# Expert output of a PEER layer: each token's v sum on four strips of 256 columns in place of two of 512

## The reference, cut to what matters

```
u = jnp.take(u_tab, ib, axis=0)                                   # 128 rows of 1024 per token
coef = gb * jax.nn.gelu(jnp.einsum('cd,ced->ce', xb, u), approximate=False)
return jnp.einsum('ce,ced->cd', coef, jnp.take(v_tab, ib, axis=0)) # the v sum of each token
```

## Time and profile before

| | |
|---|---|
| runs (us) | 3550.49, 3573.14, 3546.98 |
| profiled execution | 3567.71 us, span 3566.0, mean granted PE clock 0.855 |
| PE busy | 2750.9 us, 77% |
| DVE busy | 2363.7 us, 66% |
| POOL busy | 1964.6 us, 55% |
| ACT busy | 531.5 us, 15% |
| DMA | 1246.47 MB, mean 350 GB/s; the gathers are 1073.87 MB of it |
| line 1325 on `e_v` alone | 2844 records, 817.3 us busy |
| chain of waits that ended last | PE 36%, DVE 17%, DMA 13%, unknown queue 13%, issue 11%, POOL 7% |

### The profile page before, as it was taken

One profiled execution on the slowest core, in us unless ns is written; L12 is line 12 of the kernel. 1 busy time (PEld: TensorE's weight loads), 2 busy tenths in 40 slices (PEclk: granted clock), 3 DMA queues, 4 the chain that ended last, 5 costly groups with the idle time before them and its releaser, 6 DMA issues.

```text
span 3566.0 us, 42043 instructions
## 1 busy us (share of the span) xinstructions
PE 2750.9 (77%) x15556; PEld 1288.3 (36%) x15556; DVE 2363.7 (66%) x6100; ACT 531.5 (15%) x1162; POOL 1964.6 (55%) x2093
## 2 busy tenths in 40 slices
PE   9899886888888889986756676667656777677787
PEld 7777762333323333333323332233223332222111
DVE  5678889676676657766787767867686756665200
ACT  3211311110111102111011101010111101111101
POOL 0013345555655566556665666666665666666663
PEclk9999997999999899998867786678767787798999
DMA  6559998999999999989999999999999999999996
GB/s 218 209 179 306 352 344 305 329 359 377 382 357 322 366 375 377 369 317 403 393 373 335 369 406 368 353 338 407 379 363 332 394 395 403 386 378 396 375 361 234
DMA packets 385293, 1246.47 MB, mean 350 GB/s; under 512 B 40512, under 2 KB 75072, under 8 KB 384320
## 3 DMA queue, kind: packets, MB, share of 16 engines
q0 software_dynamic: 294912, 1073.87, 79.8%
q1 hardware_dynamic: 90176, 169.91, 13.5%
HBM read 1216.75 MB, written 26.87 MB: 349 GB/s over the span
## 4 chain that ended last, share of the span: by engine, by line
PE 36%; DVE 17%; another core or an unknown queue 13%; DMA 13%; issue 11%; POOL 7%; ACT 2%; SPq 0%; POOLq 0%; DVEq 0%; ACTq 0%
PE e_acc L1325 9%; DVE e_u L2248 5%; PE e_pl L1413 5%; DMA e_v<-in_v_tab,e_idxT 4%; DMA e_u<-in_u_tab,e_idx 3%; PE e_pd L1201 3%; PE e_pd L1021 3%; PE e_pd L1227 3%; PE e_acc L1370 3%; POOL e_v L994 3%; PE e_acc L1395 3%; DVE e_late L2248 2%; POOL e_u L986 2%; DMA e_late<-in_v_tab,e_idxT 2%
## 5 line engine op out<-in xcount | busy, mean ns | idle before, releaser
L2248 DVE CUSTOM_DVE_ANT_0 e_u<-e_u,e_c 128x1024 f32<-128x1024 f32 x776 | 942.4, 1215 | 315.8 <-DMA e_u<-in_u_tab,e_idx 240.4
L986 POOL DMA_INDIRECT e_u<-in_u_tab,e_idx x776 | 745.7, 961 | 693.3 <-DVE e_dots L2248 274.6
L994 POOL DMA_INDIRECT e_v<-in_v_tab,e_idxT x711 | 675.6, 950 | 517.4 <-PE e_acc L1325 203.3
L1325 PE MATMUL e_acc<-e_v,e_wd 128*32 128x512 f32 x2844 | 817.3, 699 | 171.6 <-DMA e_v<-in_v_tab,e_idxT 115.0
L1413 PE MATMUL e_pl<-e_late,e_v 128*128 128x512 f32 x608 | 340.8, 658 | 46.5 <-DVE e_side L2058 17.2
L2248 DVE CUSTOM_DVE_ANT_0 e_late<-e_late,e_c 128x1024 f32<-128x1024 f32 x248 | 300.8, 1214 | 102.4 <-DMA e_late<-in_u_tab,e_idx 74.3
L1325 PE MATMUL e_acc<-e_late,e_wd 128*32 128x512 f32 x832 | 271.9, 731 | 73.5 <-DMA e_late<-in_v_tab,e_idxT 47.2
L986 POOL DMA_INDIRECT e_late<-in_u_tab,e_idx x248 | 237.1, 956 | 163.8 <-DVE e_dots L2248 106.2
L1325 PEld LDWEIGHTS e_acc<-e_v,e_wd 128*32 128x32 f32 x2844 | 113.6, 116 | 533.0 <-issue 266.9
L1968 DVE SCALAR_TENSOR_TENSOR e_gbc<-e_hc,e_cw,e_gbc 128x128 f32<-128x128 f32 x960 | 303.6, 344 | 1.5 <-issue 1.0
L994 POOL DMA_INDIRECT e_late<-in_v_tab,e_idxT x208 | 197.3, 948 | 133.2 <-issue 52.8
(11 more groups left out here) (299 smaller groups left out, 3249.4 us busy)
## 6 DMA issues: line engine op xcount, KB each, us to landing
e_u<-in_w_in SPq DMA_DIRECT2D x38, 512.0 KB, 3.9
e_v<-in_w_in SPq DMA_DIRECT2D x38, 512.0 KB
e_v<-in_w_in SPq DMA_DIRECT2D x76, 256.0 KB
e_u<-in_u_tab,e_idx POOLq DMA_INDIRECT x776
e_zb<-in_w_c SPq DMA_DIRECT2D x48, 256.0 KB
e_v<-in_v_tab,e_idxT POOLq DMA_INDIRECT x711
e_arena<-in_w_r SPq DMA_DIRECT2D x32, 256.0 KB
e_zb<-in_w_r SPq DMA_DIRECT2D x32, 256.0 KB
```

The lines of the kernel that those rows point to most:

```text
L986: pool.indirect_dma_start(out=rows_in[i], out_offset=None, in_=io["u_tab"], in_offset=bass.IndirectOffsetOnAxis(ap=idx[n % 2][:, j:j + 1], ...
L994: pool.indirect_dma_start(out=rows_in[i], out_offset=None, in_=io["v_tab"], in_offset=bass.IndirectOffsetOnAxis(ap=idxT[n % (LAG + 1)][:, ...
L1325: last = pe.matmul(acc[rows, cols], w[:, at_:at_ + 32], rows_in[row][:, cols], start=(step == 0), stop=True, skip_group_check=True)
L2248: dve.tensor_tensor_reduce(rows_in[i], rows_in[i], c[:, :], 1.0, 0.0, ALU.mult, ALU.add, dots[n % 2][:, j:j + 1]).then_inc(s_dot, 1)
```

## The change

Each token's sum is cut into four parts of 256 columns, and part h goes to strip `lane ^ h`. So a token uses all four strips, with four products and eight records in place of two and four. Parts 0 and 1 share the first bank, parts 2 and 3 the second; `begins` lets only the first product of a tile in each strip and bank start afresh. The number of wait instructions per token stays, except for a tile's first token, which has four in place of two. The strip sums become 11 instructions: one of 128x256, four of 32x256, two of 64x256, four of 32x256. `HALF_SUMMED` is 5 of them, `SUMMED` all 11; who waited for the first of three now waits for five, who waited for three waits for eleven.

```diff
--- before.py
+++ after.py
@@ -158,8 +158,14 @@
 LAG, V_LAG = 1, NSEL + V_HEAD
 CHUNKS = 2
 LOW, HIGH = slice(0, P // 2), slice(P // 2, P)
-SUM_ROWS = [((slice(0, P), slice(0, P)),), ((LOW, HIGH), (HIGH, LOW))]
-SUMS = [sum(len(r) for r in SUM_ROWS[:h]) for h in range(NH + 1)]
+STRIP = P // LANES
+PARTS = LANES
+PART_W = D // PARTS
+STRIPS = [slice(STRIP * i, STRIP * (i + 1)) for i in range(LANES)]
+SUM_ROWS = [((slice(0, P), slice(0, P)),), tuple((STRIPS[i], STRIPS[i ^ 1]) for i in range(LANES)),
+            ((LOW, HIGH), (HIGH, LOW)), tuple((STRIPS[i], STRIPS[i ^ 3]) for i in range(LANES))]
+SUMS = [sum(len(r) for r in SUM_ROWS[:h]) for h in range(PARTS + 1)]
+SUMMED, HALF_SUMMED = SUMS[PARTS], SUMS[PARTS // 2]
 TAIL_AT, TAIL_SPAN, EARLY_TAILS = 4, 20, NT - 1 - LAG
 IN_PLACE = EARLY_TAILS - 1
 
@@ -169,9 +175,9 @@
     return (P // LANES) * (k % LANES) + k // LANES
 
 
-def strip_of(lane, h):
-
-    return lane ^ (2 * h)
+def strip_of(lane, part):
+
+    return lane ^ part
 
 
 ROWS = UW + VW + LW + 2
@@ -712,7 +718,7 @@
                 sp.dma_start(xin, dram["h"][n]).then_inc(s_hhin, 16)
 
             def sum_store(n):
-                sp.wait_ge(s_hh, SUMS[NH] * (n + 1))
+                sp.wait_ge(s_hh, SUMMED * (n + 1))
                 sp.dma_start(dram["h2"][n], xin).then_inc(s_h2, 16)
 
             def tail_loads(m):
@@ -1265,7 +1271,7 @@
                 if m < IN_PLACE:
                     pe.wait_ge(s_tin, 16 * (m + 1))
                 else:
-                    pe.wait_ge(s_hh, SUMS[NH] * m + (SUMS[1] if m == NT - 1 else SUMS[NH]))
+                    pe.wait_ge(s_hh, SUMMED * m + (HALF_SUMMED if m == NT - 1 else SUMMED))
                 if m:
                     pe.wait_ge(s_gp, m)
                 else:
@@ -1273,7 +1279,7 @@
                     pe.wait_ge(s_w_tail, 16 * 3)
                 if m == NT - 1:
                     turned(tail_h(m), s_ttr, range(KT // 2))
-                    pe.wait_ge(s_hh, SUMS[NH] * NT)
+                    pe.wait_ge(s_hh, SUMMED * NT)
                     turned(tail_h(m), s_ttr, range(KT // 2, KT))
                 else:
                     turned(tail_h(m), s_ttr)
@@ -1301,6 +1307,13 @@
                 product(pt, w_proj, PLE // P, 0, out)
                 product(pt, w_proj, PLE // P, 1, out).then_inc(s_pps, 1)
 
+            begun = set()
+
+            def begins(n, strip, bank):
+                first = (n, strip, bank) not in begun
+                begun.add((n, strip, bank))
+                return first
+
             def add_tokens(n, j, together):
                 if j == 0:
                     if n == 0:
@@ -1310,21 +1323,22 @@
                     pe.wait_ge(s_wd, n * (NSEL // (QUARTER * LANES)) + j // (QUARTER * LANES) + 1)
                 step = j // LANES
                 w = wd[step // QUARTER % 2]
-                for h in range(D // HALF):
+                for h in range(PARTS):
                     if j == 0 and n:
-                        pe.wait_ge(s_hh, SUMS[NH] * (n - 1) + SUMS[h + 1])
-                    cols = slice(h * HALF, (h + 1) * HALF)
+                        pe.wait_ge(s_hh, SUMMED * (n - 1) + (HALF_SUMMED, SUMMED)[h * PART_W // HALF])
+                    cols = slice(h * PART_W, (h + 1) * PART_W)
                     for i in range(together):
                         m, lane = n * NSEL + j + i, (j + i) % LANES
                         row, turn, _ = V_ROWS[m]
                         if h == 0:
                             pe.wait_ge(s_row[row], 16 * turn)
                         strip = strip_of(lane, h)
-                        rows = slice(32 * strip, 32 * strip + 32)
+                        rows = STRIPS[strip]
                         at_ = (step % QUARTER) * P + 32 * lane
-                        last = pe.matmul(acc[rows, cols], w[:, at_:at_ + 32], rows_in[row][:, cols], start=(step == 0), stop=True,
+                        last = pe.matmul(acc[rows, cols], w[:, at_:at_ + 32], rows_in[row][:, cols],
+                                         start=begins(n, strip, h * PART_W // HALF), stop=True,
                                          skip_group_check=True)
-                        if h == D // HALF - 1:
+                        if h == PARTS - 1:
                             last.then_inc(s_vmm, 1)
 
             def front(n, s):
@@ -1766,7 +1780,7 @@
                     if m < IN_PLACE:
                         act.wait_ge(s_tin, 16 * (m + 1))
                     else:
-                        act.wait_ge(s_hh, SUMS[NH] * (m + 1))
+                        act.wait_ge(s_hh, SUMMED * (m + 1))
                     if m:
                         act.wait_ge(s_outd, 16 * m)
                     else:
```

## The result

The changed kernel takes 3591.36 us (median of 8 runs, 3579.12 to 3599.93); the kernel before, beside it, 3558.03 us (8 runs, 3546.98 to 3573.14). The ratio is 1.008, interval 1.0059 to 1.0101: a little slower, within the 1% that I had called no change, and 85 us above the forecast. The profiled execution took 3579.12 us, span 3577.2, against 3567.71 and 3566.0.

A forecast was written before the change was run, and what follows sets the result against it. PE's v-sum products were taken to pace first halves, DMA transfers second halves. Terms -59 - 10 + 20 + 5 = -44 us, from 3550.5 to 3506 us; range 3440 to 3590, the forecast's own 3470 to 3530.

The forecast's parts named there:

- What bounds the kernel: In first halves of a tile's v sum PE sets the pace (tiles 0 to 2); in second halves, full DMA engines.
- The token: A token alone on PE in the v sum occupies it for 0.54 us in place of 0.98, saving 45%.
- the forecast of a third or more: Busy time of the v sum's product line on PE falls by a third or more.
- "-59" for the first halves: First halves of the v sum: 45% of the 131 us that PE's product line has in the chain is saved.
- I let the two cancel: First halves: other engines close behind PE are offset by sums hidden in the chain's 19 to 32% without named releaser.
- I take no cost for either: PE's products: doubled weight loads (0.28 us per token) and handing out eight pairs (at most 0.35 us) are hidden.
- Second halves, -10: Second halves and after 3002 us: transfers set the pace, so 10 us saved in all, ends 0 and 70.
- The strip sums, +20: Tile ends on DVE: eleven sums in place of three cost 2.5 us more, 8 times, together 20 us.
- The clock, +5: First halves of tiles 0 to 2: PE's clock share falls by 0.02, costing 5 us in the chain.
- the second rival: First halves: DVE and the recurrence's hand-overs hold the pace anyway, sums worth 0 to 15 us, about 3560 us; chance 0.22.
- the fourth rival: Strip sums decide: 0.71 us each whatever the size, 45 us on the path, 3586 to 3596 us; chance 0.13.
- the third: First halves of tiles 0 to 2: clock falls from 0.92 to 0.72, about 3558, up to 3600 us; chance 0.10.

The follow-up runs named there:

- e7: The kernel before, unchanged, traced on a faster chip: 3353.92 us.
- e8: The changed kernel with each quarter cut into two products of 128 columns, sixteen records per token, on the slower chip: 3667.55 us, ratio 1.0294 to the kernel before.
- e3: Kernel before with quarters and eleven sums in tiles 0 to 2 only, halves and three sums from tile 3, on a faster chip: 3353.34 against 3353.11 us.
- e6: The changed kernel itself, traced on a faster chip: 3355.92 us, ratio 1.0006 to the kernel before.
- e4: Kernel before with two tokens taken together in every second slot, products and sums as before, on a faster chip: 3341.48 against 3353.11 us, ratio 0.9964.
- e5: Kernel before with two tokens taken together in the odd slot instead of the even one, on a faster chip: 3362.2 against 3354.57 us, ratio 1.0026.
- e1: Kernel before with only the strip sums cut into eleven instructions, products unchanged, on a faster chip: 3364.33 against 3353.11 us, ratio 1.0035.
- e12: Repeat of the kernel before with only the strip sums cut into eleven, on a faster chip again: 3363.39 against 3353.55 us, ratio 1.0032.
- e10: Kernel before with twice the records per token, still two strips and three sums, on the slower chip: 3583.9 us, ratio 1.0061.
- e2: Kernel before with twice the records per token, still two strips and three sums, on a faster chip: 3356.74 against 3353.11 us, ratio 1.0009.
- e11: Kernel before with two tokens taken together in every second slot, on the slower chip: 3597.21 us, ratio 1.0101.

## Why the prediction was wrong

1. **What bounds the kernel: wrong in the first halves, right in the second.** I read 341 to 358 GB/s beside a PE at 85% as PE's pace. e7 has the same PE work in the same stretch and 395 GB/s, so PE was no bound at that length. What holds down on chips B stays open. The earlier trace rows could not tell: their two largest entries, "another core or an unknown queue" and "issue", are together 27 to 61% of the first halves' chain, and in a trace that lacks over a quarter of the semaphore updates they mark in large part where the chain was lost. The prediction counted the unknown queue alone (19 to 32%), and took it for a place where more of PE's work was hidden. The trace doesn't exclude that, but the time shows no saving from it.
2. **The token: right.** 0.57 us from start to start for a forecast 0.54, 8192 records, PE's busy time on `e_v` down by 23% (the forecast of a third or more was for tokens alone, and these means hold the trickling ones). The price of a record in a burst was right as well: 0.0375 us in e8, under the 0.043 of the earlier trace rows. The Trainium skill, "TensorE: Matmul & The Clock Gate", section "Wait — 56ns, not 53.3ns?", has about 62 ns per matmul with hardware decode off. The prediction held against that, but 16 records don't test it: over 100 records e8's trace has 57 ns each, the time of wide products included, and no 256 in a row are faster than 59.8 ns each. The traces neither show nor exclude such a price in a long stream, and whether hardware decode was on no run shows.
3. **In the sum, "-59" for the first halves: the step that failed.** The six first halves gave -16 us in the first trace (-5, -1, -2, -5, -4, +1), and e3 gave 0.0 on chips A, the sums of three tiles included. "I let the two cancel" was the choice: what was unnamed was not a hidden store of PE's work. On chips A the transfers take the saving, shown by e6 against e7; on chips B the saved work is idle time of PE, 166 us of it, and what PE then waits for is known in part only. What a spared PE is worth by itself no run isolates: e4 gains 12 us on chips A, and e5, with as little PE work, loses 8.
4. **"I take no cost for either", of loads and of handing out records: the second step that failed, on chips B.** On chips A twice the records are +3.6 us, within their interval of nothing; on chips B 0.61%, 22 us. The earlier trace rows is a burst of 16 records; nothing in that row prices those that come late.
5. **Second halves, -10.** They moved by +13 us together, from -7 in tile 1 to +9 in tile 4 (183 to 192), at rates within 10 GB/s of before. The strip sums lie at their ends, 2.5 us more in each, which was priced apart.
6. **The strip sums, +20: each priced right, the number on the path not.** 2.5 more each as forecast, 2.8 at the end; the eight together gave 11 and 10 us in e1 and e12. That the rest lies beside transfers that go on is argued, not measured.
7. **The clock, +5.** It fell by 0.03 to 0.06 in these halves in place of 0.02. What that cost can't be parted from the rest in the first trace; but e6 against e7 has a larger fall and no cost, and e10 has the cost and no fall.

Of the rivals, the second (something else holds the first halves, about 3560) named the outcome on chips A nearly: no difference. That the parts add up there (-12 from e4, +11 from e1 and +4 from e2 make +3, and +1 was measured) is no proof, since e5 shows that e4's gain is not the price of PE's work. On chips B the second rival names the mechanism but not the size: 0.6 to 0.8%, of which twice the records can account for all; then what the spared PE and the sums bring there cancels, within about 10 us. The measured 3591 us lies inside the 3586 to 3596 of the fourth rival, by luck: its price is refuted, 0.42 us and not 0.71. It lies inside the "up to 3600" of the third as well, but the clock of the first halves fell to 0.85 to 0.91 and not to 0.72, and e10 has the cost without the fall.

**What stays open.** What holds the kernel to 3558 to 3564 us on chips B, and why PE's records start late there. Waits of PE behind no semaphore are 42 to 240 us there and none on chips A, and for those before the v sum's products twice the records make 36 to 43 us of 3; that fits instructions that arrive late. The fetches as the profile shows them don't explain it: chips A fetch the same 155 packets with no such waits, a packet takes a median of 1.02 us in the first trace of after and 1.07 in e6, and of the 157 waits 26 end within 3 us of a packet's start, where about 20 would by chance. No run took the fetches away. The same traces are those that lack semaphore updates; whether one cause does both, no run shows. Why e11 loses 33 us there is open as well, and so is the price of eleven sums on those chips.

## What to carry to other kernels

Before a saving on an engine is valued at its share of the chain, look at the entries without a releaser. Where "issue" and an unknown queue lead the chain, its shares don't say what bounds the kernel: here a quarter of the semaphore updates was missing, and 166 us less of PE's work became 166 us more of its idle time. Waits between records that no semaphore parts, as in the token above, are the ones to take at their word. To fill idle strips of the array, take more tokens at once before cutting each into more instructions: the pairs were worth 12 us on one kind of chip, and the cut nothing there; but the slot matters (e5 lost 8), and so does the chip at hand, since on the other kind the same edit lost 33 us. An add of 256 columns from PSUM costs 0.42 us at 32 partitions as at 128, so a layout that splits partitions is paid in sums.

## What the runs showed of the hardware

The same kernel takes 3353 us on some chips and 3558 to 3564 on others, 6% apart. The gap is widest in first halves, 341 to 358 GB/s on chips B against 383 to 407 in e7, and smaller in second ones, 379 to 401 against 383 to 409. The profile's names for the waits differ too, but that is mostly its missing updates. ACT's line of the recurrence, before on chips B and e7 on chips A:

```profile
ACT e_arena L1479 <- remote: 392.0, 53, 15.6
```

```profile
ACT e_arena L1479 <- PE e_pd L1021: 376.2, 110, 14.8
```

All idle time before that line is 832 us in the first and 630 us in the second, so 202 us of it are real, and the name "remote" is not. What is PE's own there are the waits behind no semaphore, 42 us in 60 against none.

An edit's sign can hang on that: pairs give 0.9964 on one kind and 1.0101 on the other. And four strips that read one row buffer at once don't take turns: the lone token of eight records takes 0.57 us in place of 0.98.
